# Streaming encoder step on one core: the softmax scale in q's norm weight, and the first stream's keys turned beside the prompt's attention

## The reference, cut to what matters

```python
x = x + 0.5 * swiglu(rms_norm(x, ffn1_norm), ...)
h = rms_norm(x, mix_norm); proj = h @ w_in
o_gdn  = gated_deltanet(...)                      # group A, 4 heads
q = rope_partial(rms_norm(dq, q_norm), pos)       # group B, 4 heads, two maps of 64
k = rope_partial(rms_norm(dk, k_norm), pos)
s = einsum('bqhmd,bshmd->bhmqs', q, k) * (DIFF_DK ** -0.5)
p = softmax(s, axis=-1); p = p[:, :, 0] - lam * p[:, :, 1]
o_diff = rms_norm(p @ v, diff_out_norm) * (1 - lam_init)
x = x + concat(o_gdn, o_diff) @ w_out
x = x + 0.5 * swiglu(rms_norm(x, ffn2_norm), ...)
```

## Time and profile before

| | us |
|---|---|
| median of 3 runs | 1449.78 |
| lowest and highest | 1449.38, 1450.89 |
| the profiled execution's own time | 1448.19 |
| its span, first to last instruction | 1446.4 |
| TensorE busy | 1363.7 (94%) |
| VectorE busy | 896.0 (62%) |
| ScalarE busy | 676.2 (47%) |
| GpSimd busy | 364.3 (25%) |
| mean granted TensorE clock | 0.986 of full |

### The profile page before, as it was taken

One profiled execution on the slowest core, in us unless ns is written; L12 is line 12 of the kernel. 1 busy time (PEld: TensorE's weight loads), 2 busy tenths in 40 slices (PEclk: granted clock), 3 DMA queues, 4 the chain that ended last, 5 costly groups with the idle time before them and its releaser, 6 DMA issues.

```text
span 1446.4 us, 24371 instructions
## 1 busy us (share of the span) xinstructions
PE 1363.7 (94%) x8677; PEld 1237.6 (86%) x8677; DVE 896.0 (62%) x1482; ACT 676.2 (47%) x1278; POOL 364.3 (25%) x240
## 2 busy tenths in 40 slices
PE   5999999999998999999998878789999999999999
PEld 5999999988786998787777765568999999998787
DVE  5977767644446666646555766745787777754534
ACT  6555555533335453534345542543555555543332
POOL 2555555500000000121221421000555555510000
PEclk9999999999998999999999999999999999999999
DMA  6222222270100422110023016670132222244000
GB/s 197 83 83 82 80 85 87 87 296 9 29 0 19 142 75 75 59 59 29 30 74 118 1 50 199 233 262 0 59 88 87 87 87 87 87 139 181 35 2 36
DMA packets 139318, 127.27 MB, mean 88 GB/s; under 512 B 3845, under 2 KB 107909, under 8 KB 139260
## 3 DMA queue, kind: packets, MB, share of 16 engines
q1 hardware_dynamic: 136748, 117.15, 25.4%
q0 software_dynamic: 2512, 9.34, 1.9%
HBM read 115.83 MB, written 10.39 MB: 87 GB/s over the span
## 4 chain that ended last, share of the span: by engine, by line
PE 87%; DVE 8%; ACT 2%; issue 2%; DMA 0%; POOL 0%; SPq 0%; DVEq 0%; ACTq 0%
PE psum_all L943 23%; PE psum_all L944 23%; PE psum_all L945 23%; PE psum_all L953 6%; PE psum_all L1853 2%; PE psum_all L1841 2%; PE psum_all L513 1%; PE psum_all L2119 1%; PE psum_all L1845 1%; PE psum_all L1790 1%; PE psum_all L1963 1%; PE psum_all L2146 0%; DVE x_norm L463 0%; DMA x_tok<-x_prompt 0%; PE psum_all L2282 0%
## 5 line engine op out<-in xcount | busy, mean ns | idle before, releaser
L943 PE MATMUL psum_all<-hw_hi,gu_op 128*128 128x320 f32 x1200 | 372.0, 310 | 2.5 <-DVE gu_op L580 2.5
L944 PE MATMUL psum_all<-hw_lo,gu_op 128*128 128x320 f32 x1200 | 371.9, 310 | 0.0
L945 PE MATMUL psum_all<-hw_hi,gu_op 128*128 128x320 f32 x1200 | 370.9, 309 | 0.0
L943 PEld LDWEIGHTS psum_all<-hw_hi,gu_op 128*128 128x128 f32 x1200 | 226.7, 189 | 3.1 <-DVE gu_op L580 2.7
L944 PEld LDWEIGHTS psum_all<-hw_lo,gu_op 128*128 128x128 f32 x1200 | 228.1, 190 | 0.0
L945 PEld LDWEIGHTS psum_all<-hw_hi,gu_op 128*128 128x128 f32 x1200 | 226.2, 189 | 0.0
L828 POOL TENSOR_TENSOR w_sum<-raw_gu 128x512 f32<-128x512 f32 x80 | 141.0, 1762 | 225.7 <-DVE gu_op L595 221.1
L595 DVE TENSOR_TENSOR gu_op<-w_sum,gu_op 128x512 fp32r<-128x512 f32 x160 | 160.4, 1003 | 56.6 <-ACT gu_op L591 51.4
L943 PE MATMUL psum_all<-wd_hi,a_hi 128*128 128x512 f32 x440 | 171.4, 390 | 1.7 <-DVE x_tok L961 1.7
L616 DVE TENSOR_TENSOR a_lo<-aT,a_hi 128x640 fp32r<-128x640 f32 x88 | 72.6, 825 | 160.5 <-ACT a_hi L608 160.5
L944 PE MATMUL psum_all<-wd_lo,a_hi 128*128 128x512 f32 x440 | 171.2, 389 | 0.0
(11 more groups left out here) (364 smaller groups left out, 2470.0 us busy)
## 6 DMA issues: line engine op xcount, KB each, us to landing
raw_gu<-ffn_w_gu SPq DMA_DIRECT2D x80, 512.0 KB, 4.6
wd<-ffn_w_down SPq DMA_DIRECT2D x2, 4096.0 KB, 20.8
raw_b<-w_in SPq DMA_DIRECT2D x8, 1024.0 KB, 5.3
wd<-ffn_w_down SPq DMA_DIRECT2D x2, 3584.0 KB, 12.5
raw_cv<-w_in SPq DMA_DIRECT2D x13, 512.0 KB, 3.9
wd<-ffn_w_down SPq DMA_DIRECT2D x6, 1024.0 KB, 5.0
K_c<-cache_k SPq DMA_DIRECT2D x6, 1024.0 KB, 7.9
V_c<-cache_v SPq DMA_DIRECT2D x6, 1024.0 KB, 5.9
```

The costliest lines, as they stand in the source:

```text
L943: nc.tensor.matmul(out, lhs_hi, rhs_hi, start=start, stop=False, skip_group_check=True)
L944: nc.tensor.matmul(out, lhs_hi, rhs_lo, start=False, stop=False, skip_group_check=True)
L945: return nc.tensor.matmul(out, lhs_lo, rhs_hi, start=False, stop=stop, skip_group_check=True)
```

## The change

Three things:

- q's norm weight is multiplied once by minus the scale (in `qk_dve`, with a semaphore of its own), so that the scores come out as minus the scaled ones. Maxima become minima, written where the bias is read; L2162 (16 times) and L2392 (8 times) go; the exponentials have `scale=-1.0`; the mask's constant changes sign.
- The first stream's keys are turned and copied in turns 41 and 42 of `att_turns`, after the attention's own work of those turns. `att_turns` has 43 turns, and the streams' attention has no key turns of its own at its start. So the streams' attention begins in turn 113 (before: 116), and each of its steps stands three turns earlier beside delta.
- The last unit's values go to PSUM bank 4; the last OUT is written behind the turns; the first keys wait for all units but the last.

```diff
@@ qk_dve @@
             dve.wait_ge(N["params_loaded"], 16 * 9)
+            V.tensor_scalar(qk_gain[:, 0, :], qk_gain[:, 0, :], -(DK ** -0.5), None, ALU.mult)\
+                .then_inc(N["q_gain"], 1)
...
+            dve.wait_ge(N["q_gain"], 1)
             for w, x in enumerate((q_tok, k_tok)):
@@ qkT_act @@
-            nc.scalar.activation(late_neg[:], const("early_neg"), ACT.Copy)\
+            nc.scalar.activation(late_neg[:], const("early_neg"), ACT.Copy, scale=-1.0)\
@@ att_turns @@
-        def att_turns(stages):
-
-            for turn in range(START[-1] + OUT + 1):
+        FIRST_KEYS = {START[-1] + TURNED: 0, START[-1] + VALUES: 1}
+
+        def att_turns(stages, first_keys):
+
+            for turn in range(START[-1] + OUT):
                 for stage, do in stages:
                     if turn - stage in AT_TURN:
                         do(AT_TURN[turn - stage])
+                if turn in FIRST_KEYS:
+                    first_keys(FIRST_KEYS[turn])
                 yield
@@ values_out @@
+            if u == len(UNITS) - 1:
+                return psum[4][:, 0:P]
             return psum[2 * ((u + 1) % 2)][:, 0:P]
@@ att_pe @@
-            yield from att_turns(((TURN, transposes), (VALUES, values), (SCORES, scores)))
+            yield from att_turns(((TURN, transposes), (VALUES, values), (SCORES, scores)),
+                                 lambda pair: cache_keys(pe, 0, pair))
@@ att_dve: maximum @@
-                link(dve, "att_chain", MAX_LINK[u],
-                     V.tensor_reduce(soft[:, 0:2], psum_all[:, s:s + 2, 0:n], AX.X, ALU.max))
-                V.tensor_scalar(soft[:, 2:4], soft[:, 0:2], -(DK ** -0.5), None, ALU.mult)\
+                V.tensor_reduce(soft[:, 2:4], psum_all[:, s:s + 2, 0:n], AX.X, ALU.min)\
                     .then_inc(N["nmax"], 1)
@@ att_act @@
-                                         bias=soft[:, 2 + m:3 + m], scale=DK ** -0.5,
+                                         bias=soft[:, 2 + m:3 + m], scale=-1.0,
...
-            yield from att_turns(((TURNED, turned), (OUT, out), (PROBS, probs)))
+            yield from att_turns(((TURNED, turned), (OUT, out), (PROBS, probs)),
+                                 lambda pair: cache_key_act(act, 0, pair))
+            out(len(UNITS) - 1)
@@ cache_keys, out of cache_pe @@
+        def cache_keys(pe, b, pair):
+            pe.wait_ge(s_K[b % 3], (16, 16, 32)[b % 3] * (b // 3 + 1))
+            if b == 0 and pair == 0:
+                pe.wait_ge(N["pv_copied"], len(UNITS) - 1)
+            for h in (2 * pair, 2 * pair + 1):
+                n = 4 * b + h
+                if n >= 2:
+                    pe.wait_ge(N["kt_copied"], n - 1)
+                for k in range(4):
+                    last = nc.tensor.transpose(psum[2 + n % 2][:, hc(k)], K_c(b % 3, k)[:, hc(h)],
+                                               ident)
+                last.then_inc(N["kt_mm"], 1)
@@ cache_pe @@
-            pe.wait_ge(N["pv_copied"], 16)
-            keys(0, (0, 1))
-            yield
-            keys(0, (2, 3))
-            yield
             for b in range(STREAMS):
@@ cache_pe: values @@
+                if b == 0:
+                    pe.wait_ge(N["pv_copied"], len(UNITS))
@@ cache_act (cache_dve likewise) @@
-                                     scale=DK ** -0.5, accum_out=soft[:, 11:12])\
+                                     scale=-1.0, accum_out=soft[:, 11:12])\
...
-            key(0, 0)
-            yield
-            key(0, 2)
-            yield
@@ cache_dve: maximum @@
-                link(dve, "att_chain", c + 3 * b + 1,
-                     V.tensor_reduce(soft[:, 9:10], psum_flat[:, 0:PAST + STEP], AX.X, ALU.max))
-                V.tensor_scalar(soft[:, 10:11], soft[:, 9:10], -(DK ** -0.5), None, ALU.mult)\
+                V.tensor_reduce(soft[:, 10:11], psum_flat[:, 0:PAST + STEP], AX.X, ALU.min)\
                     .then_inc(N["s_nmax"], 1)
```

More of the change, by code:

```diff
@@ L2177, in combine @@
                                        ALU.mult, ALU.add).then_inc(N["pcomb"], 1)
[L2179 to L2193, removed]
+            yield from att_turns(((MAXIMUM, maximum), (COMBINE, combine)),
+                                 lambda pair: cache_key_dve(dve, 0, pair))
         def att_act(act):
@@ L2262, in cache_sync @@
                 load_values(b)
-        def cache_pe(pe):
[L2265 to L2274, removed]
+        def cache_keys(pe, b, pair):
[10 more added lines that the diff above has]
+                last.then_inc(N["kt_mm"], 1)
+        def cache_pe(pe):
             def scores(b):
@@ L2326, in cache_pe @@
                 if b + 1 < STREAMS:
-                    keys(b + 1, (0, 1))
+                    cache_keys(pe, b + 1, 0)
                 yield
@@ L2331, in cache_pe @@
                 if b + 1 < STREAMS:
-                    keys(b + 1, (2, 3))
+                    cache_keys(pe, b + 1, 1)
                 yield
@@ L2335, in cache_pe, with cache_key_act @@
             yield
-        def cache_act(act):
-            def key(b, h):
-                act.wait_ge(N["kt_mm"], 4 * b + h + 1)
-                if h == 0 and b:
-                    act.wait_ge(N["ssc_mm"], b)
-                act.wait_ge(N["kt_copied"], 4 * b + h)
-                nc.scalar.activation(KTc[:, h, :], psum[2 + h % 2], ACT.Copy)\
-                    .then_inc(N["kt_copied"], 1)
+        def cache_key_act(act, b, pair):
+            h = 2 * pair
+            act.wait_ge(N["kt_mm"], 4 * b + h + 1)
+            if h == 0 and b:
+                act.wait_ge(N["ssc_mm"], b)
+            act.wait_ge(N["kt_copied"], 4 * b + h)
+            nc.scalar.activation(KTc[:, h, :], psum[2], ACT.Copy).then_inc(N["kt_copied"], 1)
+        def cache_act(act):
             def probs(b):
@@ L2361, in cache_act @@
                 if b + 1 < STREAMS:
-                    key(b + 1, 0)
+                    cache_key_act(act, b + 1, 0)
                 yield
@@ L2371, in cache_act @@
                 if b + 1 < STREAMS:
-                    key(b + 1, 2)
+                    cache_key_act(act, b + 1, 1)
                 yield
@@ L2397, in combine @@
                 dve.wait_ge(N["s_probs"], b + 1)
-                link(dve, "att_chain", c + 3 * b + 2, V.reciprocal(soft[:, 12:13], soft[:, 11:12]))
-                link(dve, "att_chain", c + 3 * b + 3,
+                link(dve, "att_chain", c + 2 * b + 1, V.reciprocal(soft[:, 12:13], soft[:, 11:12]))
+                link(dve, "att_chain", c + 2 * b + 2,
                      V.tensor_tensor(soft[:, 13:14], soft[:, 12:13], lam[:, 6:7], ALU.mult))
@@ L2402, in combine @@
                     .then_inc(N["s_comb"], 1)
-            key(0, 1)
-            yield
-            key(0, 3)
-            yield
             for b in range(STREAMS):
@@ L2412, in cache_dve @@
                 if b + 1 < STREAMS:
-                    key(b + 1, 1)
+                    cache_key_dve(dve, b + 1, 0)
                 yield
@@ L2416, in cache_dve @@
                 if b + 1 < STREAMS:
-                    key(b + 1, 3)
+                    cache_key_dve(dve, b + 1, 1)
                 yield
```

21 lines of the change are left out of this document (11 added, 10 removed).

## The result

| | before | after |
|---|---|---|
| median of five runs, us | 1450.27 | 1458.53 |
| lowest to highest | 1449.38 to 1450.89 | 1457.33 to 1459.92 |
| the profiled execution's own time | 1448.19 | 1459.68 |
| its span | 1446.4 | 1457.9 |
| mean granted TensorE clock | 0.986 | 0.980 |

The changed kernel is slower: ratio 1.0057, with a 95% interval of 1.0045 to 1.0068, or 8.3 us. I had given 1451.4, and 1454.2 as the upper end.

What follows compares the result with a forecast made beforehand. Bound: a chain 87% TensorE, hopping between engines in turns 70 to 149. Terms -1.0 + 1.5 + 1.9 - 0.9, with rounding +1.6, took 1448.2 to 1449.8 profiled, median 1451.4 us; range 1446.0 to 1454.2.

Steps and rivals of the forecast that it cites:

- the clock term: Ahead of stream 5's turn, a 3.9 us TensorE gap lowers the clock: 1.3 us charged, bounds 0 and 2.4.
- Removed multiplications, -1.0 and 8 x 0.15: Prompt's attention gains 1.0 us, mostly at 841 us; each stream's scores lose 0.15 to 0.2 us, counted in the layout.
- the lower bound of 0.6 in my terms: At 841 us, if L1651 is held for all three GpSimd products, only L1759's 0.6 us is gained.
- The hold itself: At 841.25 us, L2162 takes 3.05 us, held while GpSimd does its three products.
- Part one, +1.5: Up to the first expansion of u: four more TensorE steps ahead of it, first `u_exp` 1.5 us later.
- part two, +1.9: The four heads: key copies and combine in u's turns make them 32.4 us instead of 30.4, +1.9.
- Part three, -0.9: From the states' end to the last copy: 40.2 us against 41.1, a gain of 0.9.
- `gdn_out`'s and `diff_out`'s collisions: Square root work before stream 4's scores costs 1.9 us; squares and sums make stream 5's maximum wait 2.7 us.
- (b): Clock falls in both gaps, ahead of stream 4's scores and stream 5's turn: 1453.5 us, chance 0.26.
- (a): Number of turns counts, VectorE's copies in the heads' loop falling into waits: faster, 1444 us, chance 0.17.
- (c): GpSimd's hold ends sooner for L1651, no fallen clock in the tail: 1448.8 us, chance 0.07.
- (d): Another wait, such as the first keys' for unit 14, keeps the old order of time: 1449.8 us, chance 0.03.

Runs made afterwards that it cites:

- Run 4: Changed kernel with idle transposes filling TensorE's gaps behind 915 us: 1452.78 us, ratio 1.0015.
- run 6: Kernel before with only the scale edit, plus idle transposes in the gaps at 845 and 858 us and behind 915 us: 1446.78 us, ratio 0.9981.
- run 13: Kernel before with only idle transposes added, in the gaps at 845 and 858 us and behind 915 us: 1448.90 us, ratio 0.9998.
- run 1: Kernel before with only the scale edit, keys and turns left as they were: 1450.95 us, ratio 1.0009.
- runs 9: Changed kernel with GpSimd's three products of the streams' tile waiting until VectorE has scaled that tile: 1454.43 us, ratio 1.0034.
- run 14: Kernel before with GpSimd's three products of the streams' tile waiting until VectorE has scaled that tile: 1445.11 us, ratio 0.9970.
- Run 7: Changed kernel with one empty turn in front of the streams' attention: 1453.68 us, ratio 1.0022.
- run 12: Changed kernel with one empty turn in delta ahead of `diff_out`: 1456.37 us, ratio 1.0040.
- 15: Changed kernel with one empty turn before the streams' attention, GpSimd's products later and `diff_out` two turns later, no idle transposes: 1446.55 us, ratio 0.9975.
- runs 10: Kernel before with only the scale edit, all idle transposes, and GpSimd's products of the streams' tile later: 1445.83 us, ratio 0.9965.

## Why the prediction was wrong

**The step that failed** is the clock term. I charged 1.3 us for one fallen clock, behind the gap ahead of turn 5, with an upper bound of 2.4, and reasoned: "it decides from a gap of about 3.9 us on, the shortest that the rows show with a fall". That the shortest gap *with* a fall is where falls begin was not read from any row. The two gaps that the rows gave, 5.29 and 3.90 us, both had a fall, so they bound the point from above and not from below. Measured: falls behind gaps of 2.35 and 2.79 us (915 and 922), behind one of 3.31 (939), and behind two of only 1.15 and 0.83 (957). The two gaps that I had priced came out shorter than laid out, 2.79 for 3.2 and 3.31 for 3.9; by my own rule neither should have brought a fall, and both did. Run 4 puts the clock's part at 5.7 us behind 915, of which I had 1.3 and nothing behind the last copy. What is left of the forecast's error then, 1452.8 against 1451.4, is inside the scatter.

Point by point:
- **Removed multiplications, -1.0 and 8 x 0.15.** The size fits at a kept clock, 2.1 us by run 6 against 13, without being shown clear of the scatter; the 0.2 for each stream is. L1651 was held for all three products, near the lower bound of 0.6 in my terms (0.46 measured). But the profiled execution lost 1.65 us again on the next 17 us (TensorE's L2135, now L2144, starts at 860.89 before and 862.08 after), since the low stretch behind the gap of 4.63 was longer than the one behind 5.29. I had taken a shorter gap to mean less of a fall. This is most of the 2.6 us of the ledger's first row, and it comes with the scale's edit in four other traces too (run 1).
- **The hold itself** I read rightly and used only as a place from which L2162 disappears. It was the largest thing there: without it both kernels are 4.1 us faster by the medians (runs 9 and 14).
- **Part one, +1.5, and part two, +1.9.** Right: 18.1 us against 17.7, 32.3 against 32.4. Run 7, with the maxima back in u's turns, took 29.5. Each head was within 0.25 us of the layout, so the sum is no luck.
- **Part three, -0.9.** The order was right, the durations were not: scores of 4 to 5 took 8.8 us for my 7.3, and of 5 to 6 10.8 for my 12. `gdn_out`'s and `diff_out`'s collisions came at the predicted places and the minimum of 5 ran at 934.70, behind the sums. But many steps between ran at the lower clock: +3.1 instead of -0.9. With the clock kept in run 4 it is 41.3, so +0.2. For the collision of `diff_out` with its slow stretch run 12 gives 2.2 us by the medians, not clear of the scatter. Two small sums of the layout don't close: the turn at 913.65 with a half of 3.8 and 1.9 more gives the scores of 4 at 919.35, not 919.15, and the four steps ahead of u in part one add up to 4.09, not 4.05.
- **Rivals.** (b) had the right sign, side and mechanism, and under a third of the excess (2.1 of 7.1 us): it counted two gaps and one stretch. (a) fell: fewer turns are not less time; three empty turns more were worth 8 us. (c) and (d) fell.
- **The scale of uncertainty.** The two profiled executions differ by 11.5 us, the medians by 8.3. One execution is a poor measure of a term of 2 us. The clock goes with that scatter: in the group of runs 13 to 15 the kernel before had a mean granted clock of 0.979 in three runs, which took 1455.8 us on average, and of 0.992 in five, which took 1447.4.

What stays open: what decides whether a low stretch behind the same gap is short or long. The gap of 4.63 us was followed by a window of 0.50 in the changed kernel and of 0.78 in run 4. And the price of the order at full clock, 5.1 by the medians or 3.6 by the ratios against 2.5 laid out, isn't told apart from scatter.

## What to carry to other kernels

When an order by turns is changed, lay out TensorE's gaps as well as its steps, and give each thin stretch half speed as the upper bound of its price: that a gap did no harm before says little, since 2.42 us did none in the kernel before and 2.35 did in the changed one. Removing waiting places from a strand can make a kernel slower, since what is gone from one place stands elsewhere, ahead of work that others wait for; here three empty turns took the loss away. And when a tiny operation shows a long duration, look at what GpSimd does at that moment and whether it could do it later: a single wait on the engine with slack was worth 4.1 us.

## What I had not expected of the hardware

- The granted clock fell to 0.50 behind gaps of 2.4 us (run 6, scores of stream 3, eight matmuls in 1.96 instead of 1.09), where the kernel before had the same gap of 2.42 at the same place and no fall. At that place the gap was 2.41 us in runs 10, 13 and 14 as well, with a fall in run 10 and none in the other two. The clock stayed up across 2.87 us in run 4. The gap's length alone doesn't decide, and no run here separates what does. The Trainium skill (TensorE: Matmul & The Clock Gate, Part 1) has the gate follow how busy TensorE has been, and the moment of the change vary between runs of one kernel; these rows fit both, but they are of different kernels, so they don't show the second by themselves.

```profile
911.98 1.96 PE L2281 MATMUL psum_all<-KTc,q_bd 128*32 128x512 f32 x8 [2.42 <-DVE KTc L2387]
```

- Idle transposes paid for themselves in the changed kernel: 5.7 us gained by 84 blocks of 128x128 that compute nothing (run 4). In the kernel before they gained 0.3, inside the scatter (run 13).
- One VectorE operation with SBUF inputs was held through three GpSimd products in a row, 3.10 us, not let in between them. The Trainium skill (SBUF — State Buffer, "SBUF: two separate sides") gives the shared ports to whoever starts first, for that whole instruction; by that rule it would have been held for one, and the measurement decides for three. Where the engines met in the middle of VectorE's work (run 14, 843 us), two of its operations took 0.50 and 1.50 us instead of 0.22 and 0.75, one product's length at most.
